# A constant 512-column product after every group of value products in attention, and two banks for the value results in place of three

## The reference

```python
s = jnp.einsum('bqhgd,bkhd->bhgqk', qblk, k, preferred_element_type=jnp.float32) * scale
p = jax.nn.softmax(s, axis=-1).astype(v.dtype)
return jnp.einsum('bhgqk,bkhe->bqhge', p, v)
```

## Time and profile before

| | |
|---|---|
| median of 3 runs | 5240.25 us |
| the profiled execution | 5242.71 us, its span 5240.9 us |
| mean granted TensorE clock over the span | 0.662 of full |
| PE busy | 2551.8 us (49%) |
| DVE busy | 2583.4 us (49%) |
| ACT busy | 789.0 us (15%) |
| POOL busy | 1333.2 us (25%) |

### The profile page before, as it was taken

How to read it: one execution, slowest core, us unless ns; L and a number is a source line. 1 busy time by engine, 2 the same in 40 slices (tenths; PEclk the granted TensorE clock), 3 DMA queues, 4 the chain that set the end, 5 groups by cost and what they waited for, 6 DMA issues and landing times. The chain is left out here.

```text
span 5240.9 us, 36566 instructions
## 1 busy us (share of the span) xinstructions
PE 2551.8 (49%) x10726; PEld 1892.2 (36%) x10726; DVE 2583.4 (49%) x4263; ACT 789.0 (15%) x1093; POOL 1333.2 (25%) x1122
## 2 busy tenths in 40 slices
PE   6599359997598259896753896710000000000001
PEld 5367237775366238771541675610000000000000
DVE  2122524322122633321324423388888888788787
ACT  2122113212022113210211322200000000000000
POOL 0010000000010000000000100001877877877875
PEclk9655579998755579998875857855555555555555
DMA  3310012223210013215223101301999999999996
GB/s 103 108 30 5 17 56 96 91 78 109 84 30 17 17 54 97 91 66 210 98 90 86 32 3 40 104 21 64 340 360 350 342 343 345 323 362 357 327 353 254
DMA packets 243145, 779.76 MB, mean 149 GB/s; under 512 B 36915, under 2 KB 49875, under 8 KB 238805
## 3 DMA queue, kind: packets, MB, share of 16 engines
q0 software_dynamic: 147456, 536.94, 28.2%
q1 hardware_dynamic: 91828, 234.68, 13.8%
q10 hardware_dynamic: 3744, 6.69, 0.3%
HBM read 744.38 MB, written 32.24 MB: 148 GB/s over the span
## 5 line engine op out<-in xcount | busy, mean ns | idle before, releaser
L1675 POOL DMA_INDIRECT sbuf<-peer_u,sbuf x512 | 647.9, 1265 | 709.5 <-issue 709.5
L108 PE MATMUL psum<-sbuf 128*128 128x512 f32 (+1 forms) x1744 | 688.6, 395 | 246.1 <-DVE sbuf L264 115.4
L1496 PE MATMUL psum<-sbuf 128*128 128x128 f32 x64 | 14.9, 379 | 1627.9 <-PEq L1645 1560.2
L1702 DVE CUSTOM_DVE_ANT_0 sbuf<-sbuf 128x1024 f32<-128x1024 f32 x512 | 620.6, 1225 | 152.0 <-DMA sbuf<-peer_u,sbuf 134.0
L1724 DVE SCALAR_TENSOR_TENSOR sbuf<-sbuf 128x1024 f32<-128x1024 f32 x512 | 657.5, 1284 | 73.3 <-DMA sbuf<-peer_v,sbuf 20.7
L109 PE MATMUL psum<-sbuf 128*128 128x512 f32 (+1 forms) x1744 | 684.6, 393 | 0.0
L110 PE MATMUL psum<-sbuf 128*128 128x512 f32 (+1 forms) x1744 | 683.4, 392 | 0.0
L932 POOL TENSOR_TENSOR sbuf<-sbuf 64x768 fp32r<-64x768 f32 (+2 forms) x22 | 29.2, 1329 | 2459.7 <-ACT sbuf L893 2459.7
L1675 POOL DMA_INDIRECT sbuf<-peer_v,sbuf x512 | 587.3, 1147 | 158.7 <-issue 158.7
L1496 PEld LDWEIGHTS psum<-sbuf 128*128 128x128 f32 x64 | 10.2, 164 | 1632.7 <-issue 1628.2
L108 PEld LDWEIGHTS psum<-sbuf 128*128 128x128 f32 x1744 | 334.4, 192 | 326.5 <-DVE sbuf L264 118.0
(11 more groups left out here) (250 smaller groups left out, 3589.6 us busy)
## 6 DMA issues: line engine op xcount, KB each, us to landing
sbuf<-w_ffn SPq DMA_DIRECT2D x88, 512.0 KB, 3.4
sbuf<-w_mod SPq DMA_DIRECT2D x12, 2048.0 KB, 8.4
sbuf<-w_fm SPq DMA_DIRECT2D x46, 512.0 KB, 3.7
sbuf<-w_down SPq DMA_DIRECT2D x16, 1408.0 KB, 6.0
sbuf<-w_out SPq DMA_DIRECT2D x24, 512.0 KB, 3.4
sbuf<-cw SPq DMA_DIRECT2D x4, 2048.0 KB, 9.8
sbuf<-wq SPq DMA_DIRECT2D x16, 512.0 KB, 3.6
sbuf<-peer_u,sbuf POOLq DMA_INDIRECT x512, 6.1
```

The costliest lines, as they stand in the source:

```text
L108: nc.tensor.matmul(acc, w_high(k), x_high(k), start=(k == 0), stop=False)
L1675: pool.indirect_dma_start(rows[:, r, :], None, table, bass.IndirectOffsetOnAxis(ap=pick[:, b, r:r + 1], axis=0)).then_inc(gathered[r], 16)
L1702: nc.vector.tensor_tensor_reduce(out=rows[:, r, :], in0=rows[:, r, :], in1=h_cur[:, :], scale=1.0, scalar=0.0, op0=ALU.mult, op1=ALU.add, ...
```

## The change

The helper that streams the constant takes its count, and is called once more after each group of value products. Its results go to a bank of their own, `spare`, which nothing reads. [...]

```diff
-def warm_up(nc, C, bank):
-
-    for _ in range(WARM):
+def multiply_constants(nc, C, bank, n):
+
+    for _ in range(n):
         nc.tensor.matmul(bank[:, :], C.ident_r[:, :], C.ident_r[:, :].unsqueeze(1).to_broadcast([P, S // P, P]),
                          start=True, stop=True)
...
-        summed = ctx.enter_context(psum(nc, [P, 3, S], F32))
+        summed = ctx.enter_context(psum(nc, [P, 2, S], F32))
+        spare = ctx.enter_context(psum(nc, [P, S], F32))
...
-                if tt == 0 and half >= 3:
-                    pe.wait_ge(taken, half - 2)
+                if tt == 0 and half >= 2:
+                    pe.wait_ge(taken, half - 1)
                 pe.wait_ge(exp_read, block0[i] + x.blocks(t))
                 for j in range(x.blocks(t)):
-                    mm = nc.tensor.matmul(summed[:, half % 3, tt * W:(tt + 1) * W], prob[0:x.kw[j], i % 2, j, t * P:(t + 1) * P],
+                    mm = nc.tensor.matmul(summed[:, half % 2, tt * W:(tt + 1) * W], prob[0:x.kw[j], i % 2, j, t * P:(t + 1) * P],
                                           v[0:x.kw[j], x.v, j, :], start=(j == 0), stop=(j == x.blocks(t) - 1))
                 if t == ST - 1:
                     mm.then_inc(pv_done, 1)
                 elif tt == NT - 1:
                     mm.then_inc(pv_half, 1)
-
-            warm_up(nc, C, row)
+                multiply_constants(nc, C, spare, 1)
+
+            multiply_constants(nc, C, spare, WARM)
...
-                got = summed[:, half % 3, 0:NT * W].rearrange("p (t d) -> p t d", d=W)
+                got = summed[:, half % 2, 0:NT * W].rearrange("p (t d) -> p t d", d=W)
```

## The result

The changed kernel took 5376.24 us (median of four runs, 5359.70 to 5383.92), against 5242.85 us before (median of four, 5238.54 to 5246.23): a ratio of 1.0246, with a 95% interval from 1.0227 to 1.0265. The profiled execution's span was 5381.8 us, 140.9 us more than before.

A forecast was written before the change was run, and what follows sets the result against it. TensorE alone was taken to bound the attentions, at the lower clock in all but the wide one. Causal 54.2, small 38.4, narrow 13 and wide 5 us sum to 111 us: 5351 us on the median, range 5333 to 5379.

The forecast's parts named there:

- TensorE's queue bounds all four attentions: All attentions: TensorE has no idle time, so constants added to its queue add their time, 111 us in sum.
- a bound that didn't come true: High bound: each constant's follower starts 0.57 us later, not 0.43, as in the `shift` pair; 22 us on 157 constants.
- 0.43 us per constant in causal and narrow items: Distance between starts at the lower clock: 126 causal constants cost 54.2 us, 31 narrow ones 13.3 us, taken as 13.
- such a balance: The constant's own weight load and the next product's load, hidden under it instead of open behind the last value product, cancel.
- Small items: 31-row groups: row-count changes make a constant between groups cost 0.70 us, an item 2.5 us; 14 items 35 us.
- Wide: Wide attention: 31 constants at 0.23 us, 7.1 us, less 2 us from closed clock dips; term 5 us (3.6 to 9).
- The ring costs nothing: Result ring of two banks: its added wait before a result's first group costs nothing; bound 2 us at 7 boundaries.
- The clock doesn't rise: Cold causal and narrow stretches: constants leave the clock low; 65-column products stay as they were. Forecast case, chance 0.72.
- the distance was not large: Clock in the cold stretches: no rise held likelier, but not by far; a rise in all would give back some 234 us.
- Rival A: Constants raise the clock in all cold 65-column stretches, if a single rise holds; 234 us back, 5085 us; chance 0.14.

## Why the prediction was right, and where it was off

- **TensorE's queue bounds all four attentions, so what is added shows.** Right. Without the constants the time was the old one, and the attentions grew by 119.2 us for 111 forecast. The rest up to 133 us isn't attributed: it lies mostly behind the last attention, where profiles scatter by 25 us. That the time still fell inside the range is in part luck. The range had its room above from a bound that didn't come true (22 us for 0.14 us more on each of 157 constants), and it was used up by the small items and by this unattributed rest, of which the forecast had nothing.
- **0.43 us per constant in causal and narrow items.** Right: the causal item grew from 11.04 to 12.75 us, 4 x 0.43. The bound above (0.57 us to the follower) is what the rows after show too, but the pair behind gives 0.15 us back. The forecast had argued for such a balance, but put it at another place: the follower's load does lie under the constant (0.14 us into it), yet behind the last value product the step is 0.40 us before and after, with nothing given back. The balance lies inside the `shift` pair (0.36 us, then 0.21).
- **Small items.** This term was mis-sized: 35 us for 14 items, 44.7 measured. That two changes of row count per constant make the surplus was confirmed by the constants of 31 rows (0.85 us for a group and its constant in place of 1.34). The step from the constant into the short products was priced from a bf16 product of 128 columns at 0.14 us above the stream; it is 0.29 above (0.72 - 0.43). The step out of them was priced at 0.13 above the records' pace of 0.22; it is 0.18 above (0.62 - 2 x 0.22). Between two groups a constant costs 1.34 - 0.44 = 0.90 us, not 0.70. The last constant of an item was priced at 0.43, and its follower starts 0.59 us later, with nothing given back. An item grew by 3.32 us where 2.5 were forecast. Layer one's part grew by 21.5 us only, not by 23.2 as layer two's, because its start, up to the second item, was 1.7 us shorter.
- **Wide: 7 us less what the dips give back.** Right in kind: 3.8 us where 5 were taken, and the clock went from 0.96 to 1.00. The forecast took work at the lower clock to last twice as long; between its own two steps, of 4.44 and 2.44 us, the factor is 1.82. The dips are gone in the profiles of the three experiments that keep one constant after each group there, and are there in the one with the ring alone. With three after each group there were dips again, so it isn't a matter of more being better, and why isn't shown.
- **The ring costs nothing.** Right, by the run of it alone.
- **The clock doesn't rise.** Right. The forecast's remark that the distance was not large held too: three constants per group raised it. The reason that it gave held only in part. It took the 65-column value products for what keeps the narrow and causal stretches low; but behind a single row the same products ran at 1.00 for 93.5 us in the causal part. They don't raise the clock, yet there they hold it. Rival A's price was right where the clock did rise: 45% less was forecast for cold stretches, and a causal item fell by 44% (11.04 to 6.21 us). Its condition was half right: a single rise did hold for the rest of the layers' attentions, as it said, but one constant after every group didn't bring the rise.
- What the forecast didn't see is the better question. The work of the causal items holds the higher clock by itself (1.00 over 93.5 us behind the row); it only never reached it. The start's 18 constants stand from 280.70 to 287.82; the clock was 0.50 to 0.51 until 286.7, then 0.99, and it was lost 3.4 us later, among the first 32- and 31-column products of the small items, with TensorE still busy all the time:

```profile
284.00:286.70 2.70, 2.70 (x8) 2.11 (x7) 0.00 (x0) 0.63 (x1) 0.82 (x1) 0.51 0.62 182
286.70:290.10 3.40, 3.40 (x20) 2.54 (x18) 0.84 (x2) 1.26 (x2) 2.98 (x3) 0.99 0.48 130
```

## What to carry to other kernels

Filler on a full engine was paid in full (0.43 us for a constant in a causal item), so price it first, and put it where it acts: a short row of it once, at the point from which the real work can hold the clock, gave 2.7%, while the same product after each group cost 2.5%. A rise and a hold are two questions (the same row of 18 raised the clock in every layer and narrow attention that had one, from 0.50 to 1.00, and it then held for 93.5 us in one and for 17 in another); look in the timeline for the last thing that ran before the clock fell. Filler between products of 31 rows should have 31 rows too: with 128 its price doubled here (0.90 us for some 0.41).

## What the runs showed of the hardware

- At the lower clock a 128-row, 512-column constant between groups of 31-row products takes 1.34 us, with 31 rows 0.85 us (group and constant together; the group alone is 0.44). In the first case the weight load behind the constant started 0.72 us after it, in the second 0.14 us.
- The granted clock fell from 1.00 with TensorE busy 6.80 of 6.80 us, among products of 31 rows, and stayed at 0.50 with it busy 203.00 of 203.00 us: its busy share in the profile doesn't tell the clock.
- The same causal item ran at 0.50 in 11.04 us or at 1.00 in 6.21 us, through fifteen items of a layer, by what had run ahead of the first of them (a row of 18 constants). With the row one item earlier, ahead of an item with 31-row value products, the clock held 6.8 us. That it was these products that lost it is argued from the two places of the row; they weren't changed by themselves.
- In the narrow attention the clock fell after 17 us in four profiles, after 31 us in one and after 41 us in one, the first and the last of these lengths with the same instructions there; with two constants per empty step it held over 94 us in two of two. What decides it wasn't taken further. Nor was a shorter row than 18 tried, or a way to have the small items run at the higher clock.
